# Modulation weights laid with their columns on the partitions, summed on VectorE, and three projections fed tile by tile

## What is computed

```python
c_act = jax.nn.silu(c)
mod = c_act @ w_ada[l] + b_ada[l]                       # 2048 x 12288 weights
sh1, sc1, gt1, sh2, sc2, gt2 = jnp.split(mod[:, None, :], 6, axis=-1)
h = rmsnorm(x, g_mix[l]) * (1.0 + sc1) + sh1
x = x + gt1 * hybrid_mixer(h, w_in[l], ...)             # pooling, attention, recurrence; then w_out
h = rmsnorm(x, g_ffn[l]) * (1.0 + sc2) + sh2
x = x + gt2 * conv_glu_ffn(h, w_ffn_gate[l], w_ffn_up[l], ..., w_ffn_down[l])
```

## Time and profile before

| what | us |
|---|---|
| median of three runs | 3135.54 |
| the profiled execution | 3136.8 |
| its span, first to last instruction | 3135.0 |
| PE busy | 3096.4 |
| DVE busy | 1981.1 |
| ACT busy | 1481.2 |

### The profile page before, as it was taken

The page is one execution under the profiler, slowest core; times in us unless marked ns, Lnnn a source line. Parts: engine busy times, 40 slices in busy tenths (PEclk is TensorE's granted clock), DMA queues, the critical chain, the costliest instruction groups (busy, mean ns, idle before and its releaser), DMA issues.

```text
span 3135.0 us, 38941 instructions
## 1 busy us (share of the span) xinstructions
PE 3096.4 (99%) x14466; PEld 2576.0 (82%) x14466; DVE 1981.1 (63%) x2086; ACT 1481.2 (47%) x1740; POOL 106.6 (3%) x206
## 2 busy tenths in 40 slices
PE   8999989999999999999999999999999999999999
PEld 7887868888888888888888888888888888888887
DVE  6778778975655655865564565556475555565564
ACT  5244535544444444545444444544545454444543
POOL 1211110100000000000000000000000000000000
PEclk9989999999999999999999999999999999999999
DMA  9978887965555555455556545555554555545555
GB/s 373 371 300 306 295 305 255 359 224 189 187 188 188 180 194 186 166 181 168 192 173 194 190 147 192 178 184 187 170 181 166 195 173 190 174 162 194 167 186 190
DMA packets 179990, 658.46 MB, mean 210 GB/s; under 512 B 20080, under 2 KB 20368, under 8 KB 179216
## 3 DMA queue, kind: packets, MB, share of 16 engines
q1 hardware_dynamic: 150992, 550.51, 52.1%
q0 software_dynamic: 28864, 106.08, 9.0%
HBM read 654.41 MB, written 2.10 MB: 209 GB/s over the span
## 4 chain that ended last, share of the span: by engine, by line
PE 96%; DMA 2%; DVE 1%; ACT 1%; issue 0%; SPq 0%; DVEq 0%; ACTq 0%
PE pg L1037 29%; PE pg L1039 29%; PE pg L1038 29%; PE pm L1072 2%; DMA w_raw<-w 1%; PE pm L1100 1%; PE pm L1558 1%; DMA R<-w_ada 1%; PE pm L1127 1%; PE pm L1452 0%; PE pm L1178 0%; PE pm L1177 0%; PE pm L1240 0%; PE pm L1135 0%; ACT w_hi L592 0%
## 5 line engine op out<-in xcount | busy, mean ns | idle before, releaser
L1607 DVE TENSOR_TENSOR w_lo<-w_raw,w_hi 128x1024 fp32r<-128x1024 f32 x888 | 1085.8, 1225 | 973.1 <-ACT w_hi L510 967.9
L510 ACT ACTIVATE w_hi<-w_raw 128x1024 fp32r<-128x1024 f32 x888 | 940.8, 1060 | 1328.5 <-PE pg L1039 1295.5
L1037 PE MATMUL pg<-w_hi,hT_hi 128*128 128x512 f32 x3232 | 1280.9, 396 | 18.5 <-DVE w_lo L1765 8.1
L1039 PE MATMUL pg<-w_hi,hT_lo 128*128 128x512 f32 x3232 | 1264.9, 391 | 0.0
L1038 PE MATMUL pg<-w_lo,hT_hi 128*128 128x512 f32 x3232 | 1264.3, 391 | 0.0
L1037 PEld LDWEIGHTS pg<-w_hi,hT_hi 128*128 128x128 f32 x3232 | 611.6, 189 | 146.4 <-issue 10.4
L1039 PEld LDWEIGHTS pg<-w_hi,hT_lo 128*128 128x128 f32 x3232 | 610.4, 189 | 129.6
L1038 PEld LDWEIGHTS pg<-w_lo,hT_hi 128*128 128x128 f32 x3232 | 611.5, 189 | 123.4 <-issue 0.5
L1037 PE MATMUL pg<-w_hi,y_parts 128*128 128x512 f32 x864 | 337.9, 391 | 1.4 <-issue 1.4
L1039 PE MATMUL pg<-w_hi,y_parts 128*128 128x512 f32 x864 | 336.4, 389 | 0.0
L1038 PE MATMUL pg<-w_lo,y_parts 128*128 128x512 f32 x864 | 336.1, 389 | 0.0
(11 more groups left out here) (281 smaller groups left out, 1380.3 us busy)
## 6 DMA issues: line engine op xcount, KB each, us to landing
w_raw<-w SPq DMA_DIRECT2D x1028, 512.0 KB, 3.7
R<-w_ada POOLq DMA_DIRECT2D x196, 512.0 KB, 7.4
R<-mem_T SPq DMA_DIRECT2D x4, 512.0 KB, 7.2
x_rows<-x SPq DMA_DIRECT2D x1, 2048.0 KB, 16.2
R<-mem_T SPq DMA_DIRECT2D x1, 2048.0 KB, 11.3
out<-x_rows SPq DMA_DIRECT2D x4, 512.0 KB, 5.8
con_sb<-con SPq DMA_DIRECT2D x1, 1344.0 KB, 16.0
small_w_sb<-small_w POOLq DMA_DIRECT2D x2, 576.0 KB, 5.8
```

Of the source, the lines that this page charges most:

```text
L510: act.activation(w_hi[:, g % RING, :, :].rearrange("p c n -> p (c n)"), raw[:, g % RING, :], ACT.Copy).then_inc(hi_done, 1)
L1037: pe.matmul(out, hi, w_hi[:, slot, c, :], start=start, stop=False)
L1039: return pe.matmul(out, lo, w_hi[:, slot, c, :], start=False, stop=stop)
L1607: tt(flat(w_lo[:, g % RING, :, :]), raw[:, g % RING, :], flat(w_hi[:, g % RING, :, :]).bitcast(F32), ALU.subtract).then_inc(lo_done, 1)
```

## The change

The modulation weights are transposed before they are loaded: a chunk is now 128 columns of `w_ada` on the partitions by 1024 of its 2048 rows along the free axis, so a block of 128 modulation values is two chunks, and there are 192. `c` is loaded once to all 128 partitions (`c_rows`, 1 MB in SBUF) and goes through Silu there. DVE takes each chunk with one `tensor_tensor_reduce`: multiply by `c_rows`, sum along the row, start from the bias or from the first chunk's sum, result in one column of `mod`. PE no longer takes part, except for the four broadcasts of the gates, now eight matmuls of 128 columns each. `h` is served in eight stages of 256 channels; scale and shift moved from DVE to ACT, which makes `hT_hi` and the fp32 copy with four instructions per stage. Tiles of `x`, `y` and `p` come in turn, three per stage (24 to 47). The first 64 chunks are weighed at feeds 2 to 42, the next 96 at feeds 44 to 130.

```diff
-AH = D // 2
+PARTS = 2
+AH = D // PARTS
...
+BANK = {"mk0": 0, "mv0": 1, "mk1": 0, "x": 1, "y": 0, "p": 2, "q0": 1, "k0": 0, "v0": 1, "q1": 0, "k1": 1, "v1": 0,
+        "o0": 1, "o1": 0, "o2": 1, "o3": 0, "mv1": 1}
+BEFORE = [max((v for v in range(u) if BANK[FRONT[v]] == BANK[FRONT[u]]), default=None) for u in range(len(FRONT))]
 F_TILES = [(u, j) for u in range(F_X) for j in range(GT)]
-F_TILES += [(u, j) for r in range(QUARTERS) for u in (F_X, F_Y) for j in (2 * r, 2 * r + 1)]
-F_TILES += [(u, j) for u in range(F_Y + 1, F_OUT) for j in range(GT)]
+F_TILES += [(F_X + i, j) for j in range(GT) for i in range(3)]
+F_TILES += [(u, j) for u in range(F_X + 3, F_OUT) for j in range(GT)]
...
+BLOCKS = [q * KD + 2 * s + c for s in range(GT) for q in (1, 0) for c in range(2)]
+M_GATE1 = len(BLOCKS)
+BLOCKS += [2 * KD + k for k in range(KD)]
+M_FF = len(BLOCKS)
+BLOCKS += [q * KD + 2 * s + c for s in range(GT) for q in (4, 3) for c in range(2)]
+M_GATE2 = len(BLOCKS)
+BLOCKS += [5 * KD + k for k in range(KD)]
+CHUNKS = [(n, h) for n in range(len(BLOCKS)) for h in range(PARTS)]
+EARLY = PARTS * M_GATE1
+ADA_PLACE = [i % len(ADA_SLOTS) if i < EARLY else (i - EARLY) % ADA_RING for i in range(len(CHUNKS))]
...
-        ada_acc = [slot(13, AH), slot(12, AH)]
+        c_rows = slot(12, PARTS, AH)
...
+        EARLY_FEEDS = [2 + 41 * i // EARLY for i in range(EARLY)]
+        READY = [max(EARLY_FEEDS[4 * PARTS * (s + 1) - 1] + 1, 20 + s) for s in range(GT)]
+
+        def front_bank(u, tb=slice(None)):
+            b = BANK[FRONT[u]]
+            return pm_all[:, 2:4, :][:, tb, :] if b == 2 else pg[b][:, tb, :]
...
+                    sp.dma_start(flat(c_rows), t["c"].partition_broadcast(P)).then_inc(c_in, 16)
...
+                if p == 0:
+                    act.wait_ge(c_in, 16)
+                    act.activation(flat(c_rows), flat(c_rows), ACT.Silu).then_inc(c_ready, 1)
...
+            def refill_mixed(s):
+
+                act.wait_ge(tile_used, 2 * GT + s + 1)
+                act.wait_ge(mod_taken, s + 1)
+                for c in range(2):
+                    k = 2 * s + c
+                    act.activation(hT_hi[:, k, :], hf_1[:, k, :], ACT.Identity, bias=mod[:, 4 * s + 2 + c:4 * s + 3 + c],
+                                   scale=mod[:, 4 * s + c:4 * s + c + 1])
+                for c in range(2):
+                    k = 2 * s + c
+                    i = act.activation(hf_1[:, k, :], hf_1[:, k, :], ACT.Identity,
+                                       bias=mod[:, 4 * s + 2 + c:4 * s + 3 + c],
+                                       scale=mod[:, 4 * s + c:4 * s + c + 1])
+                i.then_inc(hT_hi_done, 1)
...
-            def ada_sums(h, bank):
-
-                pe.wait_ge(ada_used, chunks_used(h))
-                for m in range(AH // P):
-                    i = pe.matmul(pm[bank][:, m:m + 1], ada_acc[h % 2][:, m * P:(m + 1) * P], ones[:, 0:1],
-                                  start=True, stop=True)
-                i.then_inc(acc_read, 1)
...
+                first = (M_GATE1, M_GATE1 + 8, M_GATE2, M_GATE2 + 8)[h]
+                pe.wait_ge(ada_used, PARTS * (first + 8))
+                for m in range(8):
+                    i = pe.matmul(pm[bank + m // 4][:, m % 4 * P:(m % 4 + 1) * P],
+                                  mod[:, first + m:first + m + 1].to_broadcast([P, P]), ident, start=True, stop=True)
+                i.then_inc(bc_ready, 1)
...
-            def weigh(h, k):
-
-                i = chunk_at(h, k)
-                acc, chunk = ada_acc[h % 2], ada_at[ADA_PLACE[i]]
+            def weigh(i):
...
-                if k == 0:
-                    if h >= 2:
-                        dve.wait_ge(acc_read, h - 1)
-                    if HALVES[h][0][0] in (2, 5):
-                        dve.wait_ge(ada_in[ADA_PLACE[i - 1]], 16 * ADA_TURN[i - 1])
-                        stt(acc, chunk, c_act[:, 0:1], ada_at[ADA_PLACE[i - 1]], ALU.mult, ALU.add
-                            ).then_inc(ada_used, 2)
-                    else:
-                        ts(acc, chunk, c_act[:, 0:1], None, ALU.mult).then_inc(ada_used, 1)
-                else:
-                    dve.wait_ge(ada_used, chunks_before(i, False))
-                    stt(acc, chunk, c_act[:, k:k + 1], acc, ALU.mult, ALU.add).then_inc(ada_used, 1)
...
+                start = V("b_ada")[:, n:n + 1]
+                if h:
+                    dve.wait_ge(ada_used, i)
+                    start = mod[:, n:n + 1]
+                dve.tensor_tensor_reduce(chunk, chunk, c_rows[:, h, :], 1.0, start, ALU.mult, ALU.add,
+                                         mod[:, n:n + 1]).then_inc(ada_used, 1)
+
+            def gain_stage(s):
+
+                dve.wait_ge(ada_used, 4 * PARTS * (s + 1))
+                tt(mod[:, 4 * s:4 * s + 2], mod[:, 4 * s:4 * s + 2], V("g_mix")[:, 2 * s:2 * s + 2], ALU.mult
+                   ).then_inc(mod_taken, 1)
...
-            weighs = {32 + i: [(4 + i // KD, i % KD)] for i in range(6 * KD)}
-            early = [c for c in CHUNKS if c[0] < QUARTERS and not of_pe(*c)]
-            for n, c in enumerate(early):
-                at = 2 + n if n < 12 else 14 + (n - 12) * 10 // 12 if n < 24 else 24 + (n - 24) // 3
-                weighs.setdefault(at, []).append(c)
+            weighs = {}
+            for i in range(PARTS * M_GATE2):
+                late = i - EARLY
+                weighs.setdefault(EARLY_FEEDS[i] if late < 0 else 44 + 87 * late // 96, []).append(i)
...
+            for s in range(GT):
+                if s == 5:
+                    upto(30)
+                    mem_squares(1)
                     upto(32)
-                    mem_squares(1)
-                upto(17 if r == 0 else 21 + 4 * r)
-                take_quarter(r)
-                modulated(r)
-                upto(22 + 4 * r)
-                lower_4(P_MIX + r, hf_1)
-            mem_normed(1)
-
-            upto(39)
+                    mem_normed(1)
+                upto(READY[s])
+                gain_stage(s)
+                upto(READY[s] + 1)
+                lower(P_MIX, s, hf_1[:, 2 * s:2 * s + 2, :])
...
-            upto(119)
-            take_mod(8, 0)
-            scale_gain(64, V("g_ffn"), 7)
-            upto(130)
-            take_mod(9, 1)
-            dve.wait_ge(mod_taken, 8)
-            dve.sem_inc(mod2_ready, 1)
+                lower(P_Y, 6 + q, pm[2 + q][:, :].rearrange("p (c s) -> p c s", c=2))
+            upto(131)
+            dve.wait_ge(ada_used, PARTS * M_GATE2)
+            scales = mod[:, M_FF:M_GATE2].rearrange("p (s c) -> p s c", c=4)[:, :, 0:2]
+            tt(scales, scales, V("g_ffn").rearrange("p (s c) -> p s c", c=2), ALU.mult).then_inc(mod2_ready, 1)
...
+    w_ada = a["w_ada"][0]
+    ada = [w_ada[h * AH:(h + 1) * AH, BLOCKS[n] * P:(BLOCKS[n] + 1) * P].T for n, h in CHUNKS]
```

More of the change, by code:

```diff
@@ L65 @@
 G_LAYER = G_FF + 3 * NFF
[L67 to L86, removed]
+BLOCKS = [q * KD + 2 * s + c for s in range(GT) for q in (1, 0) for c in range(2)]
[8 more added lines that the diff above has]
+ADA_PLACE = [i % len(ADA_SLOTS) if i < EARLY else (i - EARLY) % ADA_RING for i in range(len(CHUNKS))]
+ADA_TURN = [ADA_PLACE[:i + 1].count(p) for i, p in enumerate(ADA_PLACE)]
+ADA_BEFORE = [max((v for v in range(i) if ADA_PLACE[v] == p), default=None) for i, p in enumerate(ADA_PLACE)]
 IN2 = 15
@@ L714, in _ @@
                 i.then_inc(lru_act, 1)
-            upto(56)
+            upto(63)
+            for q in range(2):
+                act.wait_ge(pool_ps, q + 1)
+                act.activation(flat(pool_d[:, 2 * q:2 * q + 2, :]), pm[q][:, :],
+                               ACT.Copy).then_inc(pool_sb, 1)
             act.wait_ge(lru_dve, 2)
@@ L718, in _ @@
             act.activation(flat(TH), flat(GR), ACT.Tanh, scale=-1.0).then_inc(lru_act, 1)
-            upto(59)
+            upto(65)
+            for q in range(2):
+                act.wait_ge(pool_ps, q + 3)
+                for c in range(2):
+                    g = 2 * q + c
+                    i = act.activation(y_pool[:, g, :], pm[2 + q][:, c * S:(c + 1) * S], ACT.Copy,
+                                       scale=V("pool_scale")[:, g:g + 1])
+                i.then_inc(pool_sb, 1)
+            upto(67)
             act.wait_ge(lru_dve, 3)
@@ L1303, in _ @@
             upto(79)
-            broadcast(6, 2)
+            broadcast(0, 2)
             upto(84)
@@ L1316, in _ @@
             upto(103)
-            broadcast(7, 2)
+            broadcast(1, 2)
             upto(106)
@@ L1704, in _ @@
+            step.settle()
             L0, L1 = V("lb")[:, 0:4], V("lb")[:, 4:8]
@@ L2455 @@
     stream.append(memory[1][GT:])
-    ada = a["w_ada"][0].reshape(KD, P, ADA)
-    bias = np.zeros((P, ADA), np.float32)
-    bias[0] = a["b_ada"][0]
-    blocks = [[q * KD + first + i for q, first, n in half for i in range(n)] for half in HALVES]
-    ada = [np.concatenate([(bias if k < 0 else ada[k])[:, b * P:(b + 1) * P] for b in blocks[h]], axis=1)
```

(5 more changed lines are left out.)

352 lines of the change are left out of this document (121 added, 231 removed).

## The result

The changed kernel takes 3148.2 us (median of 5, 3146.31 to 3152.64); its time against the kernel before is 1.0039, 95% interval [1.0023, 1.0055]. That is 12.7 us over the median of before. The profiled execution took 3146.31 us with a span of 3144.5, 9.5 above before's 3135.0. Single executions of one kernel lie up to 16 us apart (beside the first experiments the kernel before took 3129.8 us at a mean granted clock of 0.992 and up to 3146.1 at 0.987), so a trace stands for its own execution.

What follows compares the result with a forecast made beforehand. PE, busy 99% of the span, was taken to bound the kernel, with DVE pacing tiles 7 to 47. Terms +4.0 + 0.8 + 5.2 + 0.5 - 10.0 = +0.5 gave 3136 us, range 3114 to 3172 for 8 in 10.

Steps and rivals of the forecast that it cites:

- the likeliest case: Whole kernel: about no change, chance 0.40; 3127 to 3146, from feed 7's start, the weighing's cost and a half-clock tile or two.
- The weighing's price, 1.30: DVE, each new weighing: 1.20 for the multiply and sum plus 0.10 for the readout; bounds 1.13 and 2.25.
- The halved rate of 2.25: Rival, DVE's weighing: the accumulator halves the rate as in the scan, 2.25 each, kernel about 3265; chance 0.08.
- The front, +4.0: Tiles 7 to 47: DVE paces, tile 46 ends at 212.7 against 209.9, loss 2.8, plus 1.2 for PE's clock.
- its eight waits: DVE in the front: behind each gain the feed waits 3.1 for ACT's `w_hi`, eight times, 24.8.
- Should ACT's waits be hidden after all, the front would gain 21.: Tiles 7 to 47: an alternative outside the sum, in which ACT's waits cost DVE nothing; gain 21.
- Tiles 48 to 131, +0.8: Middle stretch: DVE's spare time falls from 0.39 to 0.16 a feed, with only small PE waits; cost 0.8.
- a lag that peaks near 6: DVE, recurrence between feeds 54 and 69: DVE falls near 6 behind, where PE waits only beyond about 5.9.
- The last residual, +5.2: Feeds 121 to 130: DVE needs 32.4 against ten tiles' 27.2, so the last residual and PE's restart come 5.2 late.
- What goes, -10.0: PE's path: four `ada_sums` removed, 6.7, and four broadcasts each cheaper by 0.83, 3.3; together 10.0 off.
- dearer weighings (+0.5): Feed-forward layer: 32 weighings grow by 0.1 each, mostly under PE; cost 0.5.
- PE waiting for DVE in most tiles from 24 to 43: Sign in the front: PE waits for DVE in most of these tiles, with PE windows below 20 of 20 up to 200 us.

## Why the prediction was right or wrong

The time was forecast at 3136 and came to 3148.2: inside the range of 3114 to 3172, above the likeliest case's own 3127 to 3146, and on the side (slower by over 0.3%) that had a chance of 0.33. The sum was +0.5 and the trace gives +9.5. That the time fell in the range is in part luck: single terms missed by -5.1 to +9.7 and partly cancel. Term by term:

- **The weighing's price, 1.30.** Measured 1.20 alone and 1.43 in a dependent pair, 1.26 on average in the front. The halved rate of 2.25, worked out from the scan, did not come: both the old weighing and the new one, which sums as well, take 1279 ns for 1024 elements, against 1221 for a plain subtraction of the same size.
- **The front, +4.0.** Measured -1.1. Feed 7 was split at 42.5, not 45.0, and feed 43's split ended at 196.2, not 201.8; 2.5 of these 5.6 are the start, 2.4 the weighing below 1.30, the rest the smaller steps. Tile 46 ended at 209.1, not 212.7. The mechanism is shown: DVE paces, and its eight waits of 3.15 are in it (forecast 3.1).
- **"Should ACT's waits be hidden after all, the front would gain 21."** They were not hidden. Hidden by an edit of one number, they gave 19.2 in the trace and 20.9 between the medians.
- **Tiles 48 to 131, +0.8. This is the step that failed.** I treated DVE as a store of work with a lag that peaks near 6, and had it cover everything. Measured +10.5: PE waits of 2.2, 1.5, 4.7 and 0.4 make 8.9, and 1.6 is the lower clock at tile 66 and the transposes ahead of it, granted 0.54 from 295.3 to 298.9. A wait that both kernels have ahead of tile 112 (7.8 before, 6.9 now), with the slower tiles behind it (granted 0.65 before in the first 4.2 us, 0.50 now in 4.3), adds 0.6; the first set of logits gave back 1.5, and 0.9 lies in small pieces. The lag was not DVE's load alone: with 7/8 of the weighing work there left out, half of the gaps stayed. Nor was it the order of the waits alone: behind its wait of 6.1, which the order makes, DVE has no spare time up to feed 68. I had followed how ACT, DVE and PE wait for one another for the front and not for the LRU's steps, though all their `upto` numbers had moved. The 2.2 stands behind DVE's twelve convolution instructions in one block; spread over three feeds they left waits of nearly the same sum.
- **The last residual, +5.2.** PE waited 5.4 instead of 1.0, and the tile behind ran at half clock (granted 0.50 for its first 4.3 us): +6.5. Right in mechanism, 1.3 short by the clock.
- **What goes, -10.0.** The four `ada_sums`, -6.7, went. The four broadcasts, -3.3, did not get cheaper. The forecast took "x16" in the earlier trace rows for sixteen matmuls of 128 columns, where it is sixteen entries of eight, and so halved 1.78 to 0.89; measured 1.78. That is 1.8 of the miss between tiles 48 and 131. Behind tile 133 the other two broadcasts (-1.7) and dearer weighings (+0.5) were forecast, -1.2; measured +0.2.
- **PE waiting for DVE in most tiles from 24 to 43.** It waits for DVE's split ahead of six of these twenty (24, 33, 38, 40, 42 and 43). Its longest wait, 9.9 ahead of tile 25, is for ACT's evacuation of mk1's bank (`R<-pg` at 130.90), which stood behind the next gain, for which ACT waited 11.6:

```profile
127.97 1.09 ACT L669 ACTIVATE hT_hi<-R,mod 128x256 fp32r<-128x256 f32 x2 [11.62 <-DVE mod L1611]
128.97 1.08 ACT L673 ACTIVATE R<-R,mod 128x256 f32<-128x256 f32 x2
129.95 1.04 ACT L579 ACTIVATE w_hi<-w_raw 128x1024 fp32r<-128x1024 f32 x1
130.90 1.00 ACT L584 ACTIVATE R<-pg 128x1024 f32<-128x1024 f32 x1
```

I had not seen that coupling either. Behind it PE runs seven tiles without a wait while DVE's splits lie ahead of it, and has caught up at tile 33, where it waits 2.8 for DVE again. So DVE still paces the stretch; what this wait costs by itself was not tested.

Against the forecast, the failed term cost 9.7, the front gave back 5.1, the broadcasts between tiles 48 and 131 add 1.8, the last residual 1.3 and what lies behind tile 133 1.4. That is 9.1, but for rounding the distance from +0.5 to +9.5.
